# A hybrid decoder trunk on one core: split norm sums, shared key-key products, pre-added squares, and a few instructions issued in another order

## The reference, cut to what matters

```
proj = einsum('btd,dc->btc', xn, w_in)                  
# mixer B, gated DeltaNet: q, k, v go through a 4-tap convolution and silu; q and k are then normed per head
conv = silu(sum(buf[:, j:j + t_len] * cw[j] for j in range(4)))
q, k = l2n(heads(cq)) * HEAD_DIM ** -0.5, l2n(heads(ck))
kk = einsum('bhtd,bhsd->bhts', kc, kc)                    # per chunk, per head
A = eye + where(strict, bc[..., :, None] * kk * decay, 0) # solved against the right-hand sides
qk = einsum('bhtd,bhsd->bhts', qc, kc) * decay
# mixer C, HGRN2: forget-gated linear attention; its output has ONE norm over the four heads together
y_hg = rmsnorm(unheads(o_hg), hg_norm_w) * silu(hg_g)
# merge and feed-forward
merged = sum_b sigmoid(gate_b) * (y_b @ w_branch_b)
x = x + merged @ w_out;  x = x + relu(rmsnorm(x) @ w_up)**2 @ w_down
```

## Time and profile before

| | |
|---|---|
| median of 3 runs | 2112.62 us (2112.35 to 2114.3) |
| profiled execution, its time | 2113.88 us |
| its span, first to last instruction | 2112.1 us |
| TensorE busy | 2072.1 us, 98% |
| VectorE, ScalarE, GpSimd busy | 1191.9, 895.4, 939.2 us |
| mean granted TensorE clock | 0.994 |

### The profile page before, as it was taken

How to read it: one execution, slowest core, us unless ns; L and a number is a source line. 1 busy time by engine, 2 the same in 40 slices (tenths; PEclk the granted TensorE clock), 3 DMA queues, 4 the chain that set the end, 5 groups by cost and what they waited for, 6 DMA issues and landing times. The chain is left out here.

```text
span 2112.1 us, 39527 instructions
## 1 busy us (share of the span) xinstructions
PE 2072.1 (98%) x14742; PEld 2003.1 (95%) x14742; DVE 1191.9 (56%) x1892; ACT 895.4 (42%) x1704; POOL 939.2 (44%) x736
## 2 busy tenths in 40 slices
PE   7999999999999999999999999999999999999997
PEld 6999999999899999899999899999999999999996
DVE  5788434334665655234445456577554458766665
ACT  5555333333364645132333233335444445444434
POOL 2348722223211111311212222228867777988886
PEclk9999999999999999999999999999999999999999
DMA  4214546442235232365643454323444448544422
GB/s 176 74 61 131 164 147 207 123 144 89 90 115 166 76 112 69 103 199 146 196 132 109 139 189 145 130 92 137 153 143 143 158 160 267 167 134 147 136 89 88
DMA packets 229927, 287.68 MB, mean 136 GB/s; under 512 B 42190, under 2 KB 163570, under 8 KB 229670
## 3 DMA queue, kind: packets, MB, share of 16 engines
q1 hardware_dynamic: 202700, 244.70, 37.1%
q10 hardware_dynamic: 27098, 41.23, 5.3%
HBM read 194.66 MB, written 91.21 MB: 135 GB/s over the span
## 5 line engine op out<-in xcount | busy, mean ns | idle before, releaser
L452 PE MATMUL D<-xn_hi,w_hi 128*128 128x352 f32 x1992 | 660.0, 331 | 1.4 <-ACT u_in L527 0.8
L452 PE MATMUL D<-xn_lo,w_hi 128*128 128x352 f32 x1992 | 643.2, 323 | 0.0
L452 PE MATMUL D<-xn_hi,w_lo 128*128 128x352 f32 x1992 | 643.2, 323 | 0.0
L432 POOL TENSOR_TENSOR w_lo<-w_raw,w_hi 128x1024 fp32r<-128x1024 f32 (+1 forms) x105 | 242.1, 2306 | 833.9 <-ACT w_hi L426 833.9
L452 PEld LDWEIGHTS D<-xn_hi,w_hi 128*128 128x128 f32 x1992 | 374.6, 188 | 16.2 <-issue 10.9
L452 PEld LDWEIGHTS D<-xn_lo,w_hi 128*128 128x128 f32 x1992 | 374.8, 188 | 3.1 <-issue 1.9
L452 PEld LDWEIGHTS D<-xn_hi,w_lo 128*128 128x128 f32 x1992 | 374.7, 188 | 0.0
L3038 PE MATMUL PB<-x_hi,w_hi 128*128 128x264 f32 x876 | 250.2, 286 | 2.6 <-ACT stage L3074 1.8
L3038 PE MATMUL PB<-x_hi,w_lo 128*128 128x264 f32 x876 | 250.0, 285 | 0.0
L3038 PE MATMUL PB<-x_lo,w_hi 128*128 128x264 f32 x876 | 249.9, 285 | 0.0
L3038 PE MATMUL PB<-x_hi,ring_hi 128*128 128x264 f32 x860 | 244.4, 284 | 0.5 <-DVE acc L3207 0.5
(11 more groups left out here) (599 smaller groups left out, 3741.8 us busy)
## 6 DMA issues: line engine op xcount, KB each, us to landing
w_raw<-in_w_proj SPq DMA_DIRECT2D x73, 512.0 KB, 3.7
proj<-stage ACTq DMA_DIRECT2D x60, 528.0 KB, 2.8
hd<-stage SPq DMA_DIRECT2D x64, 264.0 KB, 2.5
f_rs<-hd SPq DMA_DIRECT2D x50, 264.0 KB, 2.8
stage<-hd SPq DMA_DIRECT2D x48, 264.0 KB, 2.8
w_raw<-in_w_full SPq DMA_DIRECT2D x24, 512.0 KB, 4.3
stage<-proj SPq DMA_DIRECT2D x23, 528.0 KB, 3.5
hd<-f_rs SPq DMA_DIRECT2D x32, 264.0 KB, 2.1
```

The source lines that it names most:

```text
L432: nc.gpsimd.tensor_tensor(w_lo[t.slot][:, 0:kt, :], raw(t)[0][:, 0:kt * P].rearrange("p (k m) -> p k m", m=P), w_hi[t.slot][:, 0:kt, :].bi ...
L452: last = nc.tensor.matmul(D[b][:, 0:GN], w[t.slot][:, k, :], x, start=(k == 0 and n == 0), stop=(k == kt - 1 and n == 2))
```

## The change

1. The norm sums of the convolution (L595) use split operands: ScalarE squares twice (u_q and the rounded u_qh), VectorE takes the difference u_ql ("lq"), and TensorE multiplies both by ones_r, six products with rounded operands for three fp32 ones. They stand behind the first group of the next tile instead of at the tile's end. ones_r is made at VectorE's start, no longer in `clear_gd`.
2. In `inverse_blocks` ScalarE copies the key-key products out of PSUM (b_kk, 2 copies for a head) and stores them (kkd, 512 KB for a head); VectorE's L714 reads the copy. TensorE's next head waits for that copy.
3. A DeltaNet chunk computes only the 128 columns of q; d_lt reads d_kk, which SyncE loads from kkd.
4. In an HGRN2 chunk VectorE adds the squares of four heads in two steps (q0 128x256, q1 128x128), and TensorE does one product with ones. It stands behind one more slot; the pieces are dealt out again (HG_SLOTS, and 4 slots behind it for 5), so it comes three pieces later.
5. In the HGRN2 loop the three loads of g_in are issued ahead of both weight loads.
6. In the merge ScalarE does the sigmoid ahead of `make_hi`.
7. In the feed-forward part one `up_copy` on ScalarE comes ahead of two weight splits, and two `up_difference` steps on VectorE (t4 and t6) come one place later.

The rest keeps step counts and waits in line (d_kk and b_kk get room, a wait for the stores of kkd stands in `clear_gd`). The core of the diff (left out: names of steps, buffers, HG_SLOTS, and what the order rows below show):

```diff
                 eng.activation(u_q[:, :], o, ACT.Square).then_inc(*cv_act.step(f"q{c}"))
+                eng.activation(u_qh[:, :], o, ACT.Square).then_inc(*cv_act.step(f"h{c}"))
+            if op == "lq":
+                eng.wait_ge(*cv_act.after(f"h{c}"))
+                eng.tensor_tensor(u_ql[:, :], u_q[:, :], u_qh[:, :].bitcast(F32), ALU.subtract).then_inc(*cv_dve.step(f"o{c}"))
             if op == "nq":
-                eng.wait_ge(*cv_act.after(f"q{c}"))
+                eng.wait_ge(*cv_dve.after(f"o{c}"))
                 if c:
                     eng.wait_ge(*cv_act.after(f"w{c - 1}"))
                 for g in range(TG):
-                    i = eng.matmul(M[3 + g][:, 0:GN], ones, u_q[:, cols(g)], start=True, stop=True)
+                    eng.matmul(M[3 + g][:, 0:GN], ones_r[:, :], u_qh[:, cols(g)], start=True, stop=False)
+                    i = eng.matmul(M[3 + g][:, 0:GN], ones_r[:, :], u_ql[:, cols(g)], start=False, stop=True)
...
                     for g in range(TG):
                         dense(eng, Tile(t), g, None)
+                        if g == 0 and 0 < c <= NORMED:
+                            post("nq", c - 1)
                     if 1 <= c < 1 + H:
                         inverse_blocks(kind, eng, c - 1)
-                    if c < NORMED:
-                        post("nq", c)
                 if kind == "act":
                     make_hi(eng, Tile(t + 1))
...
                     if 0 < c <= NORMED:
                         post("rs", c - 1)
+                    if 2 <= c < 2 + H:
...
                 if h:
-                    eng.wait_ge(*iv_dve.after(f"k{h - 1}{NQ - 1}1"))
+                    eng.wait_ge(*iv_act.after(f"c{h - 1}1"))
                 else:
                     rows_done(eng)
                 for n in range(NCH):
                     k = u_o[:, h % 2, n * CH:(n + 1) * CH]
                     i = eng.matmul(M[n // 4][:, n % 4 * CH:(n % 4 + 1) * CH], k, k, start=True, stop=True)
                 i.then_inc(*iv_pe.step(f"k{h}"))
+            if kind == "act":
+                eng.wait_ge(*iv_pe.after(f"k{h}"))
+                if h:
+                    eng.wait_ge(kk_st, 16 * h)
+                    eng.wait_ge(*iv_dve.after(f"k{h - 1}{NQ - 1}1"))
+                else:
+                    rows_done(eng)
+                for b in range(2):
+                    eng.activation(b_kk[:, 4 * b:4 * b + 4, :], M[b][:, :].rearrange("p (n c) -> p n c", c=CH), ACT.Copy).then_inc(*iv_act.step(f"c{h}{b}"))
+                eng.wait_ge(*iv_act.after(f"c{h}1"))
+                eng.dma_start(kkd[h].rearrange("n p c -> p n c"), b_kk[:, :, :]).then_inc(kk_st, 16)
             if kind == "dve":
-                eng.wait_ge(*iv_pe.after(f"k{h}"))
                 eng.wait_ge(*iv_dve.after("g4"))
                 for b in range(2):
+                    eng.wait_ge(*iv_act.after(f"c{h}{b}"))
                     for a in range(NQ):
                         at = (rows_of(a), slice(4 * b, 4 * b + 4), h)
-                        eng.tensor_tensor(b_l[at], M[b][rows_of(a), :].rearrange("p (n c) -> p n c", c=CH)[:, :, rows_of(a)], b_e[at],
+                        eng.tensor_tensor(b_l[at], b_kk[rows_of(a), 4 * b:4 * b + 4, rows_of(a)], b_e[at],
                                           ALU.mult).then_inc(*iv_dve.step(f"k{h}{a}{b}"))
 
         def inverse_loads(sp, part):
...
 
+                    eng.wait_ge(*act_.after("sq", n))
+                    for k in range(2):
+                        half_ = C4 >> (k + 1)
+                        if k:
+                            eng.wait_ge(*dve_.after("q0", n))
+                        eng.tensor_tensor(g_y[:, 0:half_], g_y[:, 0:half_], g_y[:, half_:2 * half_], ALU.add).then_inc(*dve_.step(f"q{k}"))
...
                 slot()
-                eng.wait_ge(*act_.after("sq", n))
-                for h in range(H):
-                    i = eng.matmul(M[3][:, 0:N], ones, g_y[:, h * N:(h + 1) * N], start=(h == 0), stop=(h == H - 1))
+                if sample:
+                    eng.wait_ge(*act_.after("sq"))
+                else:
+                    slot()
+                    eng.wait_ge(*dve_.after("q1", n))
+                for h in range(H if sample else 1):
+                    i = eng.matmul(M[3][:, 0:N], ones, g_y[:, h * N:(h + 1) * N], start=(h == 0), stop=(not sample or h == H - 1))
                 i.then_inc(*pe_.step("ss"))
...
                     eng.dma_start(hn(B.v), pcols(GD_TILE + 8, 4, col0, N)).then_inc(gx_in if sample else gd_in, 16)
+                    if not sample:
+                        if n is None:
+                            eng.wait_ge(kk_st, 16 * H)
+                        else:
+                            eng.wait_ge(*gd_dve.after("lt", n))
+                        eng.dma_start(hn(d_kk), kkd[:, bass.ds(at, 1)].rearrange("h x p c -> p (x h) c")).then_inc(gd_in, 16)
                 if sample and between != "behind":
                     token_rows()
...
                     eng.wait_ge(*gd_pool.all_of(NCH))
                 eng.wait_ge(*df.after("db", n))
-                eng.wait_ge(*pe_.after("kkqk", n))
-                eng.tensor_tensor(sq(B.lt), by_k(1), sq(B.db), ALU.mult).then_inc(*dve_.step("lt"))
+                if sample:
+                    eng.wait_ge(*pe_.after("kkqk"))
+                else:
+                    eng.wait_ge(*cols_in)
+                eng.tensor_tensor(sq(B.lt), by_k(1) if sample else sq(d_kk), sq(B.db), ALU.mult).then_inc(*dve_.step("lt"))
...
                     eng.wait_ge(*gd_dve.after("tt6", NCH - 1))
                 for h in range(H):
-                    q_and_k = B.qk[:, 0:2 * C4].rearrange("p (x h n) -> p x h n", x=2, n=N)[:, :, h, :]
-                    i = eng.matmul(MM[0:N, h * 2 * N:(h + 1) * 2 * N].rearrange("p (x n) -> p x n", n=N), hn(B.qk, C4)[:, h, :], q_and_k, start=True, stop=True)
+                    if sample:
+                        q_and_k = B.qk[:, 0:2 * C4].rearrange("p (x h n) -> p x h n", x=2, n=N)[:, :, h, :]
+                        i = eng.matmul(MM[0:N, h * 2 * N:(h + 1) * 2 * N].rearrange("p (x n) -> p x n", n=N), hn(B.qk, C4)[:, h, :], q_and_k, start=True, stop=True)
+                    else:
+                        i = eng.matmul(by_k(0)[:, h, :], hn(B.qk, C4)[:, h, :], hn(B.qk)[:, h, :], start=True, stop=True)
...
                     eng.dma_start(stage[:, s, :], proj[GATE_TILE + j0 + s], ).then_inc(gate_ld[s], 16)
                 if kind == "act":
-                    make_hi(eng, t.next(), next_kt if s == 1 else 4)
                     if j0 or s:
                         eng.wait_ge(gate_ld[s], lin(16 * (j0 // 2 + 1), 16, i))
                         eng.activation(stage[:, s, :], stage[:, s, :], ACT.Sigmoid).then_inc(gate_sig, 1)
+                    make_hi(eng, t.next(), next_kt if s == 1 else 4)
                     within(j0 + s)
                 if kind == "pool":
                     make_lo(eng, t.next(), next_kt if s == 1 else 4)
...
         UP_ADDS = [f"{what}{i}{n}" for i in (3, 4, 5) for n in range(2) for what in ("", "r")]
         UP_STEPS = UP_ADDS + ["t1", "t2", "t4", "60", "61", "t6"]
-        JOIN = UP_ADDS + "60 61 d00 d01 d10 d11 t1 d20 d21 t2 d30 d31 t4 d40 d41 t6 d50 d51 d60 d61".split()
+        JOIN = UP_ADDS + "60 61 d00 d01 d10 d11 t1 d20 d21 t2 d30 d31 d40 d41 t4 d50 d51 t6 d60 d61".split()
         f_act, f_dve, f_sq = sem("f_act"), sem("f_dve"), sem("f_sq")
...
                 w_high(act, 1, i)
             up_square(act, 0, 5)
-            for i in range(2, NCLS):
+            for i in range(2, 5):
+                w_high(act, 1, i)
+            up_copy(act, 1, 0)
+            for i in range(5, NCLS):
                 w_high(act, 1, i)
             for s in range(1, DOWN0):
                 for i in range(NCLS):
-                    if i < 3 and not (s == 1 and i == 2):
+                    if i < 3 and not (s == 1 and i in (0, 2)):
...
                     if s == DOWN0 and i == 0:
                         x_split_low(dve, 1, NCLS - 1)
-                    if s == DOWN0 and i in (1, 2, 3, 4):
-                        up_difference(dve, DOWN0 - 1, {1: 1, 2: 2, 3: 4, 4: 6}[i])
+                    if s == DOWN0 and i in (1, 2, 4, 5):
+                        up_difference(dve, DOWN0 - 1, {1: 1, 2: 2, 4: 4, 5: 6}[i])
                     if s - DOWN0 in PREPARED:
...
         LOOP_GD, LOOP_HG, LOOP_ML = GD0, GD0 + 19, GD0 + 38
         ROW_SLOTS, ML_SLOTS = [3, 6, 2, 4, 3], [3, 3, 3, 3, 3, 3]
-        HG_SLOTS = [4, 1, 2, 2, 3, 3, 3]
+        HG_SLOTS = [4, 1, 3, 1, 3, 3, 3]
...
         def clear_gd(eng):
             rows_done(eng)
+            eng.wait_ge(kk_st, 16 * H)
             eng.memset(d_S[:, :], 0.0).then_inc(ready, 1)
-            eng.tensor_copy(ones_r[:, :], ones).then_inc(ready, 1)
 
         def clear_hg(eng):
...
 
             with sp.Fori(lo, hi) as n:
+                rest = {}
+                if mixer is hgrn:
```

(4 more changed lines are left out.)

41 lines of the change are left out of this document (27 added, 14 removed).

## The result

| | before | after |
|---|---|---|
| median of 4 runs each, alternating | 2113.01 us (2112.35 to 2114.3) | 2094.69 us (2093.67 to 2095.18) |
| span of the profiled execution | 2112.1 us | 2091.9 us |
| TensorE busy | 2072.1 us | 2050.9 us |
| VectorE, ScalarE, GpSimd busy | 1191.9, 895.4, 939.2 us | 1210.2, 907.7, 939.9 us |

The ratio is 0.9915, with a 95% interval of 0.9900 to 0.9931. The change saves 18.3 us in the medians and 20.2 us between the two traces. (The two traces were not the middle runs: that of before took 0.9 us more than its median, that of after 1.0 less.) The forecast was a saving of 28.5 us, to 2084, with even odds on 2081 to 2087. 2094.7 is 7.7 us above that interval and inside the wide range of 2075 to 2095 by 0.3 us only; under two thirds of the saving came.

A forecast was written before the change was run, and what follows sets the result against it. TensorE, busy 2072.1 of 2112.1 us, was taken as the bound. Terms summed to -28.5, taking 2113.9 to 2085.4; the median, 1.3 lower, gives 2084, with 2081 to 2087 at 0.50 and a wide range of 2075 to 2095.

The forecast's parts named there:

- DeltaNet chunks: DeltaNet chunks: products of 128 instead of 256 columns save 0.83 us per chunk, 7 chunks, -5.8; d_kk's load is hidden.
- HGRN2, the loads: HGRN2 loop: g_in loads issued earlier remove waits of 7.1 us in three chunks and three clock drops, -5.1.
- HGRN2, the sum of squares: HGRN2 chunks: eight product records become two, -0.67 a chunk, 8 chunks, -5.3; bounds -5.3 and -2.
- rival 2: HGRN2 loop keeps gaps: 0.5 us in each of 8 chunks and one clock drop, +5.7, 2090; chance 0.20.
- Merge: Merge: TensorE's three gaps for L2781, 1.9 us; two go, -1.3; bounds -1.9 and -0.5.
- Two of the three go: Merge: two of TensorE's three gaps waiting for L2781 disappear, -1.3.
- Feed-forward: Feed-forward: earlier copy out of PSUM removes a 1.8 us gap and 1.6 of low clock, -3.4; later up_difference, -0.5.
- Convolution and first chunk: Convolution to DeltaNet's start: GpSimd's chain sets the start; L1969 1.6 us earlier, low clock costs 1.7, taken as 0.
- three gaps of about 1 us in c = 2 to 5: Convolution tiles c = 2 to 5, full on VectorE: gaps of about 1 us expected in three places.
- all gaps of that size here are followed by the low clock: At L1969, DeltaNet's start: a gap of about 2.2 us brings a low clock costing 1.7 us.
- Rival 1: The convolution's gain comes through, or the clock does not drop at L1969: 2080; chance 0.17.
- Rivals 3 and 4: HGRN2. 3: load order isn't the cause, +12.2, 2096, chance 0.09. 4: additions delay TensorE every chunk, over 2117, 0.04.

The follow-up runs named there:

- the padded one: Kernel before with six semaphore increments of no effect in SyncE's program at each place where the changed kernel loads d_kk, no transfer added: 2109.93 us.

## Why the prediction was right or wrong

**DeltaNet chunks, -5.8: right.** -5.8 in the traces; putting the products back cost 5.8. The load of d_kk was hidden, as said.

**HGRN2, the loads, -7.1 and -5.1: right in mechanism, and in sum partly by luck.** -12.2 forecast, -12.0 measured with the four products kept, against the very trace on which the forecast was made. The split into gaps and clock isn't a property of the kernel: a second execution of before showed 9.2 and 0, with the same total. Nor is the total: against the two other traces with this stage as before the same edit is worth 9.6 and 8.5.

**HGRN2, the sum of squares, -5.3: the term that failed most.** It came to -0.7. The prediction had named the mechanism in its bound (the eviction on ScalarE, "0.4 late in each chunk") and in rival 2, and took neither: "ss stands three pieces later, so TensorE should not wait" looked at what the additions feed, not at what stands behind them. They delay y, ScalarE waits for y ahead of its store, and the next eviction stands behind that wait. The gaps, 0.29 to 0.43 us in seven chunks, are 2.6 of the 4.6 us missing. The slow restart behind each (0.27 us beyond the idle time) makes the other 1.9: the products' starts lose 4.5 us at these seven places. With the eviction ahead of the store 5.2 of the 5.3 came.

**Merge, -1.3: the step was right and the stage wrong.** "Two of the three go" held: one gap of the three was left in the kernel before with the new order. But the kernel after has a gap of 2.9 us with a low clock (0.50 for 6.8 us) that the prediction did not see: 4.2 us lost there, 1.1 gained behind it. The step that failed is that the merge was priced by its three old gaps alone, as if the change left the arrival of y_a as it was. y_a came 2 us later, for a reason in SyncE's program that is open; the sigmoid stands behind its split. No row of before says that, except that it shows how near it was: ScalarE waited 3.7 us for y_a at 1198.11 there too.

**Feed-forward, -3.4 and -0.5: mis-sized, -1.0.** The copy went ahead and the low clock went, as said. But "the new place is two us earlier, and the gap is 1.8" took one cause for the only one. Timelines of GpSimd before and after at this place:

```profile
1456.67 1.27 POOL L2976 TENSOR_TENSOR w_lo<-s_tmp,w_hi 128x512 fp32r<-128x512 f32 x1
```

```profile
1437.49 1.27 POOL L3027 TENSOR_TENSOR w_lo<-s_tmp,w_hi 128x512 fp32r<-128x512 f32 x1
```

Before, this w_lo ended at 1457.94, 0.42 us ahead of TensorE's start behind the gap (1458.36). After, the copy starts at 1436.49 and TensorE still waits until 1438.82, 1.44 us, for that w_lo. The gap shrank by 0.4. The rest was given back later, at 1460:

```profile
1459.23 0.29 PE L3089 MATMUL PB<-x_hi,ring_lo 128*128 128x264 f32 x1
1460.09 0.36 PE L3089 MATMUL PB<-x_hi,w_hi 128*128 128x264 f32 x1 [0.57 <-ACT stage L3125]
```

There ScalarE waited 4.7 us before its copy; this wait moved the following products by 0.8 us. The later up_difference brought nothing: the wait of 0.55 us at 1770.60 went (0.6 us with its restart), and two new ones came at 1757.26 and 1775.27 (0.2 and 0.5). In starts of products these make 0.3 + 1.6 - 0.8 + 0.6 - 0.7 = 1.0 us, what was measured.

**Convolution and first chunk, 0: -2.0.** The main reason held: GpSimd's chain sets the start (run without the low part: both 1.1 earlier), two late w_lo cost 1.46 us (1.5 forecast), and the gap at L1969's like was 1.66 (2.2 forecast). The start came 1.8 us earlier (1.6 forecast), but that it came so near is luck. The chain ended 1.7 us earlier and not 0.8 (whose own terms, -1.8 + 2.1 - 0.8, give 0.5). ones_r gave 0.16 us and not 0.77: VectorE does not run "without a pause" to d_vb but waits 1.35 us for ScalarE's d_de in both kernels, behind a step that was now longer. And the three gaps of about 1 us in c = 2 to 5 did not come; a wait for u_ql and one for u_in (0.62 us), both by 107 us, took their place, so that TensorE's lead behind the last norm sum was 4.1 us (3.8 forecast). The step that failed is "all gaps of that size here are followed by the low clock": this one was not, in the trace of after. In the other kernels it sometimes was (below). Besides, u_ql costs GpSimd's chain about 0.6 us each, not 1.0. Rival 1's second half, "the clock does not drop at L1969", is what happened, without rival 1's gain.

**882 us, not forecast: -1.6.** The kernel before ran at a clock of 0.83 in 880 to 890 us with no gap ahead; the trace of after did not. Both executions of before had it and so did the padded one; the one with the merge's new order, the same program up to there, did not, so it varies between executions. Of the kernel after and its variants three of thirteen had it, just the three with the eviction ahead of the store. With one trace of most kernels it isn't shown whether the change took it away or chance did.

Summing up: the HGRN2 squares missed by 4.6 us, the merge by 4.4 and the feed-forward by 2.9; the convolution (2.0) and the 882 us (1.6) gave some of it back; with 0.2 of the loads that is the 8.5 us between -28.5 and -20.0. Rival 2 was right on the gaps and its price of them (4.0, measured 4.5), but its clock drop did not come: no HGRN2 window was below 1.00. Of rival 1 only the clock at L1969 held. Rivals 3 and 4 are excluded.

## What to carry to other kernels

When work is added to an engine, ask not only who needs its result, but which waiting instruction stands behind it on another engine and what that engine would have done next: here a store's wait on ScalarE held back a PSUM eviction, and moving one slot turned -0.7 into -5.2. Before a gap is booked as gain, look for the second-latest thing it waits for: a gap closes only down to that one. When a small gap opens, add the restart to its price (0.27 us here). Book a low clock behind a gap as a chance, not as a price, and take a second trace of the kernel before where much hangs on it.
